# A convolution gate's inverse on GpSimd in place of VectorE, in a fused attention, convolution and expert layer

## The reference

```python
h = rms_norm(x, g_mix);  q, k, v, f, a, gate = split(h @ w_in)
attn = fox_attention(q, k, v, log_sigmoid(f + b_f))          # 8 heads of 64, causal
u = a * sigmoid(gate)                                        # conv_module
y = layer_norm(depthwise_conv(u, w_dw) + b_dw, ln_g, ln_b)   # 31 taps, 512 channels
conv = silu(y)                                               # y / (1 + exp(-y))
x = x + concat(attn, conv) @ w_out
x = x + peer_ffn(rms_norm(x, g_ffn))                         # 8 heads x 16 gathered experts per row
out = rms_norm(x, g_final)
```

## Time and profile before

| | us |
|---|---|
| median of 3 runs | 3469.15 (3465.49 to 3469.71) |
| the profiled execution, its own time | 3473.65 |
| its span, first to last instruction | 3471.7 |
| PE busy | 2483.2 |
| DVE busy | 2488.9 |
| ACT busy | 996.6 |
| POOL busy | 1454.8 |

### The profile page before, as it was taken

One profiled execution on the slowest core, in us unless ns is written; L12 is line 12 of the kernel. 1 busy time (PEld: TensorE's weight loads), 2 busy tenths in 40 slices (PEclk: granted clock), 3 DMA queues, 4 the chain that ended last, 5 costly groups with the idle time before them and its releaser, 6 DMA issues. The chain is left out here.

```text
span 3471.7 us, 41167 instructions
## 1 busy us (share of the span) xinstructions
PE 2483.2 (72%) x13379; PEld 1018.3 (29%) x13379; DVE 2488.9 (72%) x6867; ACT 996.6 (29%) x2816; POOL 1454.8 (42%) x1266
## 2 busy tenths in 40 slices
PE   7999889676667666766766676667666766766764
PEld 4444666422222222222222222222222222222221
DVE  4888678677677767776776777777777766767885
ACT  3333444322232222222222222222222222222331
POOL 2333231144444444444444444444444444535443
PEclk9999889798888888888888888878888888888877
DMA  4000200799999999999999999999999999999997
GB/s 154 27 24 21 75 31 19 276 421 421 420 412 419 420 413 418 415 416 417 416 415 416 411 412 418 419 413 416 417 419 414 413 419 416 402 366 421 413 421 328
DMA packets 194557, 1198.43 MB, mean 345 GB/s; under 512 B 31051, under 2 KB 41379, under 8 KB 55102
## 3 DMA queue, kind: packets, MB, share of 16 engines
q0 software_dynamic: 156672, 1140.92, 79.8%
q1 hardware_dynamic: 37694, 55.13, 4.6%
HBM read 1181.14 MB, written 14.84 MB: 344 GB/s over the span
## 5 line engine op out<-in xcount | busy, mean ns | idle before, releaser
L1311 PE MATMUL ps<-uv_rows,diag 64*64 64x512 f32 x8704 | 1355.1, 748 | 898.7 <-ACT diag L1433 896.9
L1220 POOL DMA_INDIRECT uv_rows<-in_uv_emb,experts x1088 | 1287.0, 1183 | 1510.2 <-PE ps L1311 1304.2
L1582 DVE CUSTOM_DVE_ANT_0 uv_rows<-uv_rows,xn_c 128x1024 f32<-128x1024 f32 x1088 | 1332.7, 1225 | 740.1 <-DMA uv_rows<-in_uv_emb,experts 734.7
L1311 PEld LDWEIGHTS ps<-uv_rows,diag 64*64 64x64 f32 x8704 | 325.4, 154 | 1638.8 <-ACT diag L1433 1206.7
L1425 ACT ACTIVATE gelu_c<-dots 128x2 f32<-128x2 f32 x544 | 110.7, 204 | 1754.1 <-DVE dots L1582 1753.9
L1433 ACT ACTIVATE diag<-ident_twice,act_c 128x64 f32<-128x64 f32 x1088 | 319.2, 340 | 286.6 <-DVE act_c L1599 285.9
L1274 PE MATMUL ps<-w_pq_sb,xnT_c 128*128 128x256 f32 x1152 | 350.5, 435 | 1.2 <-ACT xnT_c L1395 1.2
L1274 PEld LDWEIGHTS ps<-w_pq_sb,xnT_c 128*128 128x128 f32 x1152 | 223.0, 211 | 270.5 <-issue 246.8
L577 DVE SCALAR_TENSOR_TENSOR convT<-w_out_sb,tapsT,convT 128x128 f32 (+1 forms) x960 | 252.8, 343 | 0.0
L517 PE MATMUL ps<-w_in_sb,w_out_sb 128*128 128x512 f32 (+1 forms) x656 | 241.7, 524 | 12.2 <-ACT w_out_sb L403 12.2
L339 POOL TENSOR_TENSOR rstd_a<-ms_a,neg_half 128x1 f32<-128x1 f32 x9 | 85.6, 9509 | 181.1 <-ACT ms_a L384 181.1
(11 more groups left out here) (208 smaller groups left out, 2100.9 us busy)
## 6 DMA issues: line engine op xcount, KB each, us to landing
uv_rows<-in_uv_emb,experts POOLq DMA_INDIRECT x1088, 12.6
w_in_sb<-in_w_in SPq DMA_DIRECT2D x4, 2048.0 KB, 11.7
w_pq_sb<-in_w_pq SPq DMA_DIRECT2D x8, 1024.0 KB, 12.0
cat_turned<-catT SPq DMA_DIRECT2D x9, 512.0 KB, 2.6
w_out_sb<-in_x_prompt SPq DMA_DIRECT2D x8, 512.0 KB, 3.6
w_out_sb<-in_w_out SPq DMA_DIRECT2D x1, 4096.0 KB, 16.0
catT_c<-cat_turned SPq DMA_DIRECT2D x8, 512.0 KB, 8.0
out<-x_c SPq DMA_DIRECT2D x8, 512.0 KB, 8.2
```

Of the source, the lines that this page charges most:

```text
L1220: nc.gpsimd.indirect_dma_start(out=rows[:, m % RING, :], out_offset=None, in_=d.uv_emb[0], in_offset=bass.IndirectOffsetOnAxis(ap=experts[ ...
L1311: ins = pe.matmul(ps[dst, 2 * x + half, :], diag[src, (m + i) % DIAGS, :], rows[src, (m + i) % RING, cols], start=first, stop=last)
L1582: nc.vector.tensor_tensor_reduce(out=row, in0=row, in1=xn[:, block_of(n) % 2, :], scale=1.0, scalar=0.0, op0=ALU.mult, op1=ALU.add, accum_ ...
```

## The change

The reciprocal of the gate leaves DVE. POOL waits for ACT's exponential of a block (`gate_ready`), adds one, and raises the result to the power of minus one, where the exponent is a small tile of minus ones, read with a stride of zero along the rows. It does so for block `b - 1` at the start of block `b`, ahead of that block's layer norm operations and taps, and once more behind the last block. DVE waits for the new semaphore `inverse_ready` in front of the product, and the product moves from head 3 to head 5 of the next block (it stays at head 3 where that is the sample's block).

```diff
+        inverse_ready, neg_one_ready = sem("inverse_ready"), sem("neg_one_ready")
+        neg_one = sb("neg_one", [P, s.CCH])
...
+            def inverse_gate(b):
+                pool.wait_ge(gate_ready, b + 1)
+                chain.link(nc.gpsimd.tensor_scalar(gate[:, :, :], gate[:, :, :], 1.0, None, ALU.add))
+                nc.gpsimd.tensor_tensor(out=gate[:, :, :], in0=gate[:, :, :],
+                                        in1=neg_one[:, :].unsqueeze(2).broadcast_to([P, s.CCH, P]), op=ALU.pow).then_inc(inverse_ready, 1)
+
+            nc.gpsimd.memset(neg_one[:, :], -1.0).then_inc(neg_one_ready, 1)
+            pool.wait_ge(neg_one_ready, 1)
             pool.wait_ge(zeros_ready, 1)
...
             for b in range(BLOCKS):
+                if b > 0:
+                    inverse_gate(b - 1)
                 pool.wait_ge(mv_ready, b + 1)
...
                     for j in range(b * TAPS_A_BLOCK, min((b + 1) * TAPS_A_BLOCK, s.TAPS)):
                         tap(j)
+            inverse_gate(BLOCKS - 1)
...
-            def inverse_gate(b):
-                dve.wait_ge(gate_ready, b + 1)
-                chain.link(nc.vector.tensor_scalar(gate[:, :, :], gate[:, :, :], 1.0, None, ALU.add))
-                chain.link(nc.vector.reciprocal(gate[:, :, :], gate[:, :, :]))
-
             def silu(b):
+                dve.wait_ge(inverse_ready, b + 1)
                 if b >= 2:
                     dve.wait_ge(cat_stored[b % 2], 16 * (b // 2))
...
-                if h == 2 and b > 0:
-                    inverse_gate(b - 1)
-                if h == 3 and b > 0:
+                if h == 5 - 2 * (b == s.NB) and b > 0:
                     silu(b - 1)
                 if h == conv_at(b, 7):
                     hold(b)
-            inverse_gate(BLOCKS - 1)
             silu(BLOCKS - 1)
```

## The result

The changed kernel takes 4145.72 us (median of 4 runs, 4144.33 to 4153.17) against 3468.42: ratio 1.1955, 95% interval 1.1941 to 1.1968. It is 677 us slower.

A forecast was written before the change was run, and what follows sets the result against it. PE, with gaps waiting for DVE's probabilities, was taken to bound the attention stage. Eight blocks at X - 4.7 and the tail at X - 3.1 gave +184 us on 3469: 3653 us, range 3440 to 4300 for 8 in 10.

The forecast's parts named there:

- The sign and the place: Slower, by 184 us, chance of slower 0.74; placed in the attention stage, with the expert stage's length held fixed.
- the likeliest mechanism: Attention stage: GpSimd's power holds the shared ports, blocking DVE's next multiply through all of X; 3537 to 3969, chance 0.33.
- X: Duration of one GpSimd power over 128x512 in the gate's inverse, taken as 25 us.
- the middle: Middle by ratio, 18 us, between the two ends for one wide power, 1.85 and 178.7 us.
- the forecast's own sum: Attention stage: eight blocks at X - 4.7 plus the tail at X - 3.1, 9X - 40.6; +184 us.
- second rival: Attention stage: DVE runs on beside the power until the layer norm's scale; +135, 3604 us; chance 0.12.
- third rival: GpSimd's wide power: no column overlaps the next, X of 60 to 179 us, 3969 to 5040; chance 0.20.
- its slack: Second rival, each block: DVE works on 8.2 us before the layer norm's scale stops it, so late by X - 8.2.
- What went: DVE loses nine adds and nine reciprocals, 33.9 us; of that the path had 21.5 us, PE's eight waits.
- the tail's wait: Behind the last block, the ninth gate's product starts at 627.7 + X in place of 630.82: X - 3.1.
- first rival: GpSimd's power streams like an add, X of 1.85 to about 4.5 us; 3432 to 3446, likely 3440; chance 0.25.

The follow-up runs named there:

- the two orders that were run: The changed kernel, 4145.72 us; and the changed kernel with the layer norm's add and power ahead of the gate's on GpSimd, 4171.85 us.
- with the product: The changed kernel with GpSimd's wide power replaced by a product of the same shape and operands, constant tile 0.0: 3431.66 us, ratio 0.9891.

## Why the prediction was wrong

The sign and the place held; the size of one term did not, nor did the likeliest mechanism.

- **The term that was mis-sized** is X: "So I go above the middle and take X = 25 us, which is 49 ns a column, a seventh of that extra." It is 82 us, 159 ns a column, nearly half of the 0.346 us that the one-column power showed over a subtraction. Nearest in kind, that row deserved more than a step above the middle. Put into the forecast's own sum it gives 9 x 82.1 - 40.6 = +698, 4167 us, within 21 of what was measured. That does not speak for the sum's mechanism: the second rival's sum lies only 50 us lower, whatever X is. The third rival had X in its span. The range held the time because it reached to X of 97, not because of the X or the mechanism that it was drawn around.
- **The mechanism that failed** is "So a long power makes DVE's next multiply wait until it ends." Of the rows from which it was argued, one pair shows a hold by an add of 0.72 us, the other a power held back by DVE, which is the other direction. The wide power takes 79 times as long as a product of as many columns (82 us against 1.04), and multiplies run beside it at their usual length. That it reads too seldom to hold the ports, as the second rival has it, fits; the reason itself was not isolated. The rule of the Trainium skill (SBUF — State Buffer, section "Who interferes with whom"), that the second to come waits for the whole of the first, does not agree for this instruction: 320 multiplies at a median of 0.486 us, all beside an 82 us power.
- **The second rival was what happened**: DVE runs on to the scale and stops there. With X = 82.1 its sum is 8 x (82.1 - 10.9) + 79 = +649; measured +677. The 28 missing are its slack, the time that DVE works on before it stops. I took it from one block with wide heads, 8.2 us; the mean of the eight waits, 77.4 us, leaves 4.7, and 8 x 3.5 is 28. The second block, with narrow heads, waited 80.41, the sample's, whose scale comes two heads earlier, 82.36, the eighth 72.92; and the add took 1.5 where I had 0.7.
- **What went** was right: PE's waits for the probabilities 25.2 to 4.4, the product's move nothing (3472.98), the tail's wait up by 79.3 against X - 3.1 = 79.0.
- **The first rival's price** was right as a price: with a cheap operation in the same place, 3431.66 against 3432 to 3446.
- **Two rows were misread**, without a change to the sum. The 0.75 us called a plain product is the row of a sum (L741). And the powers of one column did not cost the same each time: the nine of L753 took 557 to 931 ns.

The decision between slower by 184 and by 677 hung on one number that the trace had at one column only. No run was needed to know which end was dangerous; one run of a wide power would have settled it.

## What to carry to other kernels

An operation's row at one column prices its start and one step (here 0.38 and 0.16 us); before it is used on hundreds of columns, what repeats per column has to be measured, and where it can't be, the extra over a plain operation of the same shape was nearer here (346 ns against 159) than the middle (35). An idle engine hides work only up to the length of the loop that it is put into: 82 us cannot hide in a block of some 31, and the two orders that were run lost 677 and 703 us. If the aim is to relieve the busiest engine, the engine with the cheap primitive is the one to try: three passes of 0.63 us on ACT, one of them there before, and two table loads a block made the kernel 28 us faster.

## What the runs showed that I had not expected

- GpSimd's power costs 0.38 us and 159.4 ns a column on 128 partitions, by one line through 1, 256 and 512 columns; the product of the same operands over 512 columns took 1.04 us.
- GpSimd's add of a constant over 512 columns takes 1.50 us, longer than that product with two inputs.
- DVE's multiplies are held by a short operation of GpSimd (0.29 us became 0.81 behind an add of 0.72), but not by its power of 82 us.
- Of what relieving DVE gave, more than half came through PE's clock (20.2 of 37 us with the product, 16.5 of 28 with the inverse on ACT): busy time for the same matmuls was 218.8 us at 0.86, 209.6 at 0.91, 202.3 at 0.93 and 198.6 at 0.95, and time and clock multiply to 188 to 191 in all four.
